# A decoder layer on eight cores: another order for the first loads, for the second half of the cross-attention, and for the last products

## The reference, cut to what matters

```
h    = rms_norm(x, ln_mix_w);  proj = h @ w_in              # 12800 columns
o_att = dilated sliding-window attention (3 groups x 4 heads), merged over the groups
o_hg  = chunked gated recurrence (8 heads), normed and gated
x = x + (sigmoid(gate_a) * (o_att @ w_branch_a) + sigmoid(gate_b) * (o_hg @ w_branch_b)) @ w_out
hc = rms_norm(x, ln_cross_w);  mn = rms_norm(mem, ln_mem_w)
qc = hc @ wq_cross             # 4 heads of 128
kc, vc = mn @ wkv_cross        # 256 memory tokens
oc = softmax(qc kc^T / sqrt(128)) vc;   x = x + oc @ wo_cross
hf = rms_norm(x, ln_ffn_w);    x = x + (silu(hf @ w1) * (hf @ w3)) @ w2      # 5632 wide
y  = rms_norm(x, ln_final_w)
```

## Time and profile before

| | before |
|---|---|
| three runs | 2279.42, 2282.6, 2527.74 us; median 2282.6 |
| profiled execution | 2280.11 us, span of its slowest core (6) 2278.4 us |
| spans of cores 0 to 7 | 2278.3, 2274.3, 2273.6, 2275.6, 2273.4, 2275.3, 2278.4, 2274.7 us |
| granted TensorE clock, mean | 0.994 on cores 0 and 6, 0.995 to 0.997 on the others |
| TensorE busy | 2205.7 us, 97% of the span |
| VectorE, ScalarE, GpSimd busy | 35%, 25%, 8% |

### The profile page before, as it was taken

How to read it: one execution, slowest core, us unless ns; L and a number is a source line. 1 busy time by engine, 2 the same in 40 slices (tenths; PEclk the granted TensorE clock), 3 DMA queues, 4 the chain that set the end, 5 groups by cost and what they waited for, 6 DMA issues and landing times.

```text
span 2278.4 us, 36013 instructions; the slowest of 8 cores (2273.4 to 2278.4 us)
## 1 busy us (share of the span) xinstructions
PE 2205.7 (97%) x14656; PEld 1188.7 (52%) x14656; DVE 802.0 (35%) x1287; ACT 562.6 (25%) x939; POOL 179.9 (8%) x217
## 2 busy tenths in 40 slices
PE   4899999999999999999999989999999999999998
PEld 2676766766656664444444444444444444444443
DVE  2543222245555552111113462224324314414416
ACT  3442111145555552111112562000000000000014
POOL 0000000001011112222210000000000000000000
PEclk9999999999999999999999999999999999999999
DMA  9754453130431408363695317444444444444323
GB/s 230 180 142 75 75 88 52 30 57 2 74 54 22 70 5 172 52 102 51 99 188 79 75 19 148 74 74 74 74 74 75 74 75 75 74 84 80 70 45 148
DMA packets 61616, 188.72 MB, mean 83 GB/s; under 512 B 3472, under 2 KB 36240, under 8 KB 45456
## 3 DMA queue, kind: packets, MB, share of 16 engines
q0 software_dynamic: 53968, 145.01, 38.4%
q1 hardware_dynamic: 7488, 41.43, 5.2%
HBM read 323.04 MB, written 8.39 MB: 145 GB/s over the span
## 4 chain that ended last, share of the span: by engine, by line
PE 87%; DVE 6%; ACT 4%; issue 2%; DMA 1%; DVEq 0%; SPq 0%; ACTq 0%
PE P L306 86%; DVE hU L899 1%; DMA R<-xo 1%; DVE R L897 1%; DVE R L808 1%; PE P L372 1%; ACT R L804 1%; PE P L1089 1%; DVE R L839 0%; ACT L804 0%; DVE R L361 0%; ACT L763 0%; DVE R L814 0%; ACT R L357 0%; DVE R L802 0%
## 5 line engine op out<-in xcount | busy, mean ns | idle before, releaser
L306 PE MATMUL P<-hT,wb 128*128 128x512 bf16 (+1 forms) x6016 | 1328.3, 378 | 2.2 <-DVE hT L317 1.4
L306 PEld LDWEIGHTS P<-hT,wb 128*128 128x128 bf16 x6016 | 580.6, 98 | 671.1 <-issue 7.4
L306 PE MATMUL P<-wb,hT 128*128 128x128 bf16 (+1 forms) x6464 | 717.4, 272 | 5.6 <-DVE R L317 2.9
L306 PEld LDWEIGHTS P<-wb,hT 128*128 128x128 bf16 x6464 | 462.6, 108 | 256.5 <-issue 7.1
L1054 DVE TENSOR_TENSOR R<-R,P 128x512 f32<-128x512 f32 x384 | 262.7, 687 | 151.7 <-PE P L306 150.8
L1269 DVE TENSOR_TENSOR hT<-P,tmp 128x512 bf16<-128x512 f32 x88 | 60.9, 692 | 538.2 <-PE P L306 538.2
L1268 ACT ACTIVATE tmp<-P 128x512 f32<-128x512 f32 x88 | 52.5, 597 | 782.0 <-PE P L306 781.9
L1010 DVE TENSOR_TENSOR tmp<-P,R 128x512 f32<-128x512 f32 x64 | 44.3, 691 | 246.7 <-PE P L306 246.7
L285 POOL DMA_DIRECT2D wb<-w x66 | 39.3, 596 | 905.5 <-PE P L306 895.2
L994 ACT ACTIVATE R<-P 128x512 f32<-128x512 f32 x64 | 38.2, 597 | 249.7 <-PE P L306 249.7
L306 PE MATMUL P<-R,wb 128*128 128x512 bf16 (+1 forms) x448 | 95.9, 365 | 0.0
(11 more groups left out here) (116 smaller groups left out, 989.7 us busy)
## 6 DMA issues: line engine op xcount, KB each, us to landing
wb<-w POOLq DMA_DIRECT2D x66, 1024.0 KB, 10.9
wb<-w_in POOLq DMA_DIRECT2D x50, 1024.0 KB, 15.1
R<-xo SPq DMA_DIRECT2D x16, 1024.0 KB, 12.9
R<-xp SPq DMA_DIRECT2D x8, 1024.0 KB, 6.3
wb<-w_out POOLq DMA_DIRECT2D x8, 1024.0 KB, 19.4
y<-R SPq DMA_DIRECT2D x14, 512.0 KB, 2.8
wb<-wkv_c POOLq DMA_DIRECT2D x4, 1024.0 KB, 15.4
wb<-w_bb POOLq DMA_DIRECT2D x8, 512.0 KB, 9.6
```

What stands on the lines that cost most here:

```text
L306: P.pe(lambda e: e.matmul(out, lhsT, rhs, start=start, stop=stop, skip_group_check=skip), reads=reads, writes=writes)
```

## The change

Three places are changed.

1. Front: w0 waits for x2 and w1 for x3. One logarithm of a constant is put ahead of the first norm. In unit 0 the norms of x4 to x7 stand earlier in the order, their transposes a little later.
2. Cross-attention: scores and products of the heads of the second half stand between `q_proj` and `wo_tile` 0 to 3; `hn_tr(0)` stands behind `wo_tile(1)`, `hn_tr(1)` behind `wo_tile(3)`.
3. End: for t = 7, GpSimd multiplies the first three pieces of x by the weight as soon as their squares are taken. Behind the scale, ScalarE scales 1024 columns, VectorE forms the last 512 as before and scales 512. There are three stores, the last of 512 KB.

```diff
-            gate = {1: [XK[2]], 2: wkey(0), 3: wkey(1), 4: wkey(2), 5: wkey(3)}
+            gate = {0: [XK[2]], 1: [XK[3]], 2: wkey(0), 3: wkey(1), 4: wkey(2), 5: wkey(3)}
...
         W = att_load(0)
+        P.act(lambda e: e.activation(out=dummy[:, 7:8], in_=epsc[:], func=AF.Ln), reads=["epsc"], writes=["dummy7"])
...
+                    first = [(8.0, lambda: xnorm(4)), (11.0, lambda: xnorm(5)), (14.5, lambda: (xtr(4), xnorm(6))),
+                             (18.0, lambda: (xtr(5), xnorm(7), xin(8))), (20.8, lambda: (xtr(6), xin(9))), (22.8, lambda: xtr(7)),
+                             (26.0, lambda: (xnorm(8), xin(10)))]
...
         wo_tile(0)
+        c_score(0, 1, (2, 3))
         q_proj(2, 1)
+        c_pv(0, 1)
         wo_tile(1)
+        c_score(1, 1, (2, 3))
+        hn_tr(0)
         q_proj(3, 1)
-        c_score(0, 1, (2, 3))
+        c_pv(1, 1)
         wo_tile(2)
-        c_pv(0, 1)
-        c_score(1, 1, (2, 3))
+        c_score(2, 1, (2, 3))
         wo_tile(3)
-        c_pv(1, 1)
-        c_score(2, 1, (2, 3))
+        c_pv(2, 1)
         rstd_x(3, 2)
+        c_score(3, 1, (2, 3))
+        hn_tr(1)
         hn_scale(3)
-        hn_tr(0)
-        hn_tr(1)
-        c_pv(2, 1)
-        c_score(3, 1, (2, 3))
         hn_tr(2)
         c_pv(3, 1)
         hn_tr(3)
...
+                if t == 7 and nb < 3:
+                    P.pool(... out=xr, in0=xr, in1=rowf[...], op=ALU.mult ...)
...
         rstd_x(7)
-        for i in range(4):
-            store(7, i * 512, 512)
+        P.act(... out=xs[:, 7, 0:1024], in_=xs[:, 7, 0:1024], func=AF.Copy, scale=r7 ...)
+        store(7, 1536, 512)
+        P.dve(... tensor_scalar(out=xs[:, 7, 1024:1536], in0=xs[:, 7, 1024:1536], scalar1=r7, op0=ALU.mult) ...)
+        for c0, n in ((1024, 512), (0, 1024)):
+            P.dma("sp", ... out=y[7 * 128:8 * 128, c0:c0 + n], in_=xs[:, 7, c0:c0 + n] ...)
```

More of the change, by code:

```diff
@@ L672, in build @@
             if u in NST:
-                ns = steps([nstep(i) for _, i in NST[u]][:5] + [lambda: (xnorm(8), xin(10))] + [nstep(i) for _, i in NST[u]][5:]) if u == 0 \
-                    else steps([nstep(i) for _, i in NST[u]])
-                ev += [(t, 0, ns) for t in sorted([t for t, _ in NST[u]] + ([26.0] if u == 0 else []))]
+                if u == 0:
+                    first = [(8.0, lambda: xnorm(4)), (11.0, lambda: xnorm(5)), (14.5, lambda: (xtr(4), xnorm(6))),
+                             (18.0, lambda: (xtr(5), xnorm(7), xin(8))), (20.8, lambda: (xtr(6), xin(9))), (22.8, lambda: xtr(7)),
+                             (26.0, lambda: (xnorm(8), xin(10)))]
+                else:
+                    first = []
+                lst = first + [(t, nstep(i)) for t, i in NST[u] if not (u == 0 and i < 8)]
+                ns = steps([f for _, f in lst])
+                ev += [(t, 0, ns) for t, _ in lst]
             if u == 4:
@@ L1334, in build @@
                 sq_x(t, nb)
+                if t == 7 and nb < 3:
+                    xr = xs[:, 7, nb * 512:(nb + 1) * 512]
+                    P.pool(lambda e, xr=xr, nb=nb: e.tensor_tensor(out=xr, in0=xr, in1=rowf[:, nb * 512:(nb + 1) * 512], op=ALU.mult),
+                           reads=[("x", 7, nb), "rowf"], writes=[("x", 7, nb)])
                 if t > 0:
@@ L1340, in build @@
         rstd_x(7)
-        for i in range(4):
-            store(7, i * 512, 512)
+        r7 = rsv[:, 7:8]
+        P.act(lambda e: e.activation(out=xs[:, 7, 0:1024], in_=xs[:, 7, 0:1024], func=AF.Copy, scale=r7),
+              reads=[("x", 7, 0), ("x", 7, 1), ("rs", 7)], writes=[("x", 7, 0), ("x", 7, 1)])
+        store(7, 1536, 512)
+        P.dve(lambda e: e.tensor_scalar(out=xs[:, 7, 1024:1536], in0=xs[:, 7, 1024:1536], scalar1=r7, scalar2=None, op0=ALU.mult),
+              reads=[("x", 7, 2), ("rs", 7)], writes=[("x", 7, 2)])
+        for c0, n in ((1024, 512), (0, 1024)):
+            ks = [("x", 7, i) for i in range(c0 // 512, (c0 + n) // 512)]
+            P.dma("sp", lambda e, c0=c0, n=n: e.dma_start(out=y[7 * 128:8 * 128, c0:c0 + n], in_=xs[:, 7, c0:c0 + n]),
+                  reads=ks, writes=[("y", 7, c0)])
         P.emit(st)
```

## The result

| | before | after |
|---|---|---|
| time, median | 2282.2 us (16 runs) | 2312.9 us (16 runs); 2291.2 us in a second series of 7 |
| ratio of the runs compared | | 1.0065 [1.004, 1.009]; second series 1.0037 [1.0025, 1.005] |
| profiled execution | 2280.11 us | 2287.86 us |
| slowest core and its span | 6, 2278.4 us | 0, 2285.6 us |

What follows compares the result with a forecast made beforehand. TensorE holds 87% of the chain of waits, so gains come only where it idles or runs at half clock. Front +1.5, cross-attention +3.5, end -0.5 give +4.5 on the profiled 2280.1 us: 2284.6, put at 2285, range 2272 to 2293.

Steps and rivals of the forecast that it cites:

- Front, first tiles: Start of the kernel: x1 to x3 come alone, first projection at 32.8 us, so PE starts 6.1 us earlier.
- Front, the tiles behind: Front, x4 to x7: tiles land every 10.0 us beside weights, x7 8 us later than it was; +1.5 us for the slowest core.
- so all cores come out near the same place: Front: core 6 loses 1.4 us, others some 5 us, cores 2 and 4 with 4.8 and 5.0 in hand; +1.5 for the slowest.
- up to 2 us more: Front: bound for PE perhaps running at half clock behind its new wait of 6 us.
- The rule weighed there: Front: DMA engines alternate queues packet by packet, so x tiles would take 9.2 us, x7 landing at 68.8; 10.0 was kept.
- Cross-attention: Waits of 3.2 us ahead of hn_tr(0) and 6 us ahead of hn_tr(2); +3.5 us, bounds 0 and +6.
- End: End of the kernel: shorter work behind the scale, but 1 MB still goes through the queue; -0.5 us, between -1 and 0.
- GpSimd's three products lie beside the last two pieces: End: products of 1.27 us each run beside ffn_down's last two pieces; uncovered, the last would cost 1.27 us.
- the last store is issued about 1 us earlier: End: VectorE's 2.74 us become 0.69 + 0.54, with ScalarE's 1.24 beside it, so the last store's issue comes about 1 us earlier.
- A: Rival, front: x is not late and the 6.1 us stay; 2271 to 2277 us, decided by x7 landing by 66; chance 0.26.
- B: Rival, cross-attention: the tail's 8.8 us are won as well; 2261 to 2265 us together with A; chance 0.06.
- C: Rival: three new front waits and two in cross-attention each bring a 1.2 GHz spell, x tiles at 10.5 us; 2294 us; chance 0.12.

Runs made afterwards that it cites:

- e1: Only the front of the change (gates, early logarithm, norms further ahead) on the kernel before: 2286.7 us, ratio 1.0019 [1.0008, 1.0029].
- e2: Only the cross-attention order of the change on the kernel before: 2287.1 us, ratio 1.0017 [1.0008, 1.0027].
- e7: Only the change's cross-attention on the kernel before, with hn_tr(0) moved behind q_proj(3, 1) and c_pv(1, 1): 2282.3 us, ratio 0.9996 [0.9985, 1.0006].
- e3: Only the end of the change on the kernel before: 2284.5 us, ratio 1.0019 [0.9997, 1.004].
- e8: Only the change's end on the kernel before, with GpSimd's three products left out: 2282.9 us, ratio 0.9999 [0.999, 1.0008].
- e14: Front of the change with w3 waiting for x10's landing, w4 and w5 behind it; rest as before: 2275.7 us, ratio 0.9967 [0.9954, 0.998].
- e15: e14's front plus e11's cross-attention order, end as in the kernel before: 2273.6 us, ratio 0.9961 [0.9946, 0.9976].
- e11: e9's cross-attention order with wo_tile(5) moved ahead of the first ffn_up, front and end as before: 2279.0 us, ratio 0.9987 [0.9978, 0.9997].
- e6: Front of the change with weight tile w3 waiting for x6 in place of w1: 2284.1 us, ratio 1.0000 [0.9991, 1.001] against the kernel before.
- e9: Kernel before with another cross-attention order, heads' scores and products spread, hn_tr(3) behind wo_tile(4): 2285.4 us, ratio 1.0012 [1.0002, 1.0022].

## Why the prediction was right and wrong

**The sign and the mechanisms were right.** x tiles late, x7 deciding, a new wait ahead of `hn_tr(0)`, a longer one ahead of `hn_tr(2)`: each is in the trace. The forecast of 2285 is 4 us under the 2289.3 that the change sets, and the range to 2293 holds that. It does not hold the median of all 16, 2312.9: nine executions lie at 2309.8 and above, and the sum has no term for what made them long, which no run here explains. Of the 4 us, some 2 lie in the base: I added the +4.5 to the profiled execution of 2280.1, which stood 2.5 us under the median. Added to 2282.6 it gives 2287.1. The other 2 to 3 are in the terms: 4.5 forecast, 7.3 on core 0.

**Front, first tiles:** right. Projection at 34.00 on core 0 and at 32.6 to 33.5 on the others (forecast 32.8).

**Front, the tiles behind: the term that was mis-sized,** +1.5 forecast, +2.6 on core 0 at `wo_tile(0)`, +4 by e1 (interval 1.8 to 6.6). On core 6, the one the step was worked out for, x7's sum starts at 72.00 (forecast 72.3) and its transposes at 77.62 (77.5). What failed is "so all cores come out near the same place". Cores 0 and 6 were the slow ones before since only they had spells at half clock in this stage, and that hid what the tiles cost the others. At `wo_tile(0)` core 6 is 0.4 us earlier, but cores 2, 4, 5 and 7 are 7.7, 6.8, 5.8 and 6.1 later, against the "some 5 us" that I gave them and the 4.8 and 5.0 they had in hand. Two things stand behind this. x4 took 15 us from its issue on core 0, not 10.0, since nothing of it moved for the first 4. And the clock fell most where it had been up: from 1.00 to 0.78 on the six other cores, from 0.89 on cores 0 and 6.

The range named the second, "up to 2 us more". The first was to be had from the trace: x6, issued behind a queued weight tile at 41.74, took until 55 by the prediction's own rows, 13 us and not 10.5. The window of 44.5 to 55 left the time behind the issue out.

The rule weighed there gave 68.8 us for the landing of x7. By the Trainium skill, "DMA: Bandwidth & Descriptors", section "Queues, rings and completion order", each DMA engine takes turns packet by packet between the queues that it has work for. The trace agrees from 37.5 us on (138 packets against 137), and in the first 4 us behind the issue it has 73 packets of weights and none of x; whether the engines had work of x by then, no row tells. Keeping 10.0 us a tile was nearer: x7's sum at 71.1 to 75.1.

**Cross-attention: right.** +3.5 forecast, +4.2 on core 0, +3.9 by e2. The waits were 2.88 (3.2) and 5.63 (6). Two things in the working are off. The 5.2 us of work put ahead of `wo_tile(2)` are 3.1 by the prices given there (five pairs of products and 16 transposes more), and only so do its own 1323.8 come out; `wo_tile(2)` did end 7.7 us later against `wo_tile(0)`, as forecast. And the loss is paid by the first wait alone, as e7 shows, not "by the new wait and by the longer last one".

**End: wrong sign.** -0.5 forecast, +0.6 on core 0, unclear by the runs of e3. Two steps failed. "GpSimd's three products lie beside the last two pieces": they do, but not for free, as e8 shows. That stretches the norm ahead of the last add, which starts 0.94 us later behind the last matmul (0.4 us were won between `wo_tile(4)` and there). And "the last store is issued about 1 us earlier" is true and brought nothing on core 0: 9.14 us from the add to the end in both. The prediction had the reason, all of the 1 MB goes through the queue behind the first piece and this piece comes no earlier, and took -0.5 all the same. For the first step the Trainium skill has a rule that I passed over: "SBUF — State Buffer", section "Who interferes with whom", says that a VectorE operation with two inputs in SBUF contends with a GpSimd operation that reads SBUF, and that the ports they share are an exclusive lock. The trace agrees in kind. VectorE began at 2272.54 with 0.70 us of GpSimd's product left, and took 0.51 longer; GpSimd began at 2273.58 with 0.75 of VectorE's left, and took 0.60 longer; the adds, with one input in PSUM, kept their 0.67 to 0.69 us beside it.

**The rivals.** A (x not late) fell: it decided at 66 us, and x7's sum began at 71.1 or later. Its gain was real, though: e14 and e15 got it with a gate that the change lacks. B's won tail was never in this change; e11 has a part of it. C, slower still from 2293 on, came near in its mechanism, five waits with spells at 1.2 GHz behind the long ones, and not in its time.

## What to carry to other kernels

When a load is held back to let another pass, list what else is in flight until the last tile of that stage has landed. Here three tiles won 5 to 6 us and the four behind them lost it to weights that were needed much later; holding those back as well turned +4 us into -7, though they then came up to 3 us late themselves. When a wait goes, look for the next reader of the same data: e6 and e9 moved their wait some 12 and 10 us down the program, past the mark I was watching. And for the slowest of eight cores, price a change on each of them: the slowest before may be slow for a reason that the others only get with the change, as here the lower clock in the front.

## What the runs showed of the hardware

- A 1 MB tile of x issued while weight tiles were queued moved no packet for 4 us (core 0, from 31.44). In e14, without weights in flight, the first packets moved within 1 us of the issue and the tile took 5.1 us (core 3). Beside weights a tile followed the one before by 9.4 to 9.7.
- A VectorE product of two SBUF operands, 128x1024, took 1.69 and 1.79 us beside a GpSimd product, 1.27 without; GpSimd's own went from 1.26 to 1.78 and 1.87.
- Behind the waits of 2.88 and 5.63 us the clock was at its lower level: 16 transposes took 1.86 us, and 1.06 us where TensorE had been busy. In e14's stage on core 0, with waits of 1.61 us at most, it stayed at 1.00. A wait of 2.53 us in e14 (core 3, up to 53.05) was followed by 0.50, and one of 2.94 (core 3, up to 112.41) by 1.00.
